# One projection of a two-layer block on Trainium2: seven half-width block products instead of eight, with the weight sums on GpSimd

## The chip, the core and the metric

The kernel runs on one core of a Trainium2 chip (trn2). The metric is the device time of one execution in microseconds (us); lower is better. Three executions of the kernel before took 1381.69, 1382.02 and 1382.20 us; their median is 1382.02 us. Engines: PE is TensorE, DVE is VectorE, ACT is ScalarE, POOL is GpSimd, SP is SyncE, which here only issues DMAs.

## What is computed

Two transformer layers over 512 tokens of width 1024, float32 in and out. The first layer has a gated linear attention and a dilated attention and then this feed-forward part, the only one that the change touches:

```python
nm = rmsnorm(h, mlp_norm_g[l])
a = jnp.square(jax.nn.relu(jnp.einsum('bsd,df->bsf', nm, w_ff1[l])))
h = h + jnp.einsum('bsf,fd->bsd', a, w_ff2[l])
```

The hidden width is 4096.

The second layer (stick-breaking attention, HGRN2, a gated feed-forward part) follows and ends the kernel.

## The kernel before, in words

**Layout.** Activations lie transposed: a row of 128 features on the partitions, 512 tokens (S) along them. `hT` holds the residual stream h as 8 such rows.

**Three products for one.** Every large product is made of rounded operands (float32r). A weight W is split in a high part `WH` (rounded) and a low part `WL` = W - WH; an activation X in `XH` and `XL` likewise. Each 128 x 128 block of weights costs three matmuls: WH·XH, WH·XL and WL·XH (lines 538, 542, 545, the inner lines of `products` in `tensor`).

**Units and pieces.** `Plan` (lines 99 to 209) cuts all weights in units of 256 output columns over 8 blocks of 128 rows. A unit is two tiles (`t`), each of which accumulates 8 blocks in one PSUM bank of 512 tokens: 2 x 8 x 3 = 48 matmuls of 128 x 512. The weights of a unit come in two pieces of 4 blocks (1024 columns, 512 KB). Plan gives each tile a time in units of three matmuls (one block); the other engines' work is ordered by such times. A generator yields the time at which its next instruction is due, and `merge` (lines 72 to 82) sorts the streams of one engine by them. These times fix only the order in each engine's queue: on the chip an instruction starts when the one before it and the semaphores that it waits for let it.

**The way of a piece.** SP loads it from HBM into one of three `RAW` buffers (line 1925). ACT rounds it into one of `HL` = 5 `WH` buffers (line 861, `splits`), once the piece five before it has been used by PE (`("product", "block", ...)`). ACT then writes the negated high part into `WL` (line 869, `negated`), and POOL issues a DMA that adds the original weight from HBM onto it (line 1881, `lows`, `accum_op=ALU.add`). This addition is done by the DMA engines, so each piece is read from HBM twice. `split_time` and `low_time` give the times of these steps, from the time at which the piece five before is used.

**The first feed-forward part.** 4096 hidden features in four groups of 1024. For group g, stage `("f1", g)` (4 units of `w_ff1`) gives 8 rows; `relu2` takes each out of PSUM on DVE (line 1572), squares it (line 1062) and rounds it (line 1064) on ACT into `AH1`, and subtracts on DVE (line 1575) for `AL1`. Stage `("f2", g)` (4 units of `w_ff2`) multiplies by these and adds each tile to `hT` on DVE (line 1559, `to_h`). Products go round three PSUM banks `GB`; four more, `FB`, serve the attention stages.

Of the kernel before, what the change touches and what calls it, by code (L numbers as in the profile page):

```python
# [29 lines left out]
DOWN = [(0, 8), (8, 16), (16, 22)]  # L30

# [53 lines left out]
class Tile:  # L85


    def __init__(self, g, u, c, i, st, kt, cols, sets, v0, v1):
        self.g, self.u, self.c, self.i, self.st = g, u, c, i, st
        self.kt, self.cols, self.sets, self.v0, self.v1 = kt, cols, sets, v0, v1  # L90

# [7 lines left out]
class Plan:  # L99
# [3 lines left out]
    def __init__(self):  # L103
# [16 lines left out]
        for g in range(4):  # L120
            add(("f1", g), "w_ff1", 4 * g, 4 * g + 4, 8, UC)
            add(("f2", g), "w_ff2", 4 * g, 4 * g + 4, 8, UC)
# [16 lines left out]
        for u, (st, name, i, kt, cols, k0) in enumerate(units):  # L139
            self.first.append(len(self.pieces))  # L140
            n = max(1, PIECE // cols)
            ends = [0, 1, 2, 4, 6, 8] if u == 0 else [*range(0, kt, n), kt]
# [7 lines left out]
        paired = {0, next(u for u, unit in enumerate(units) if unit[0] == "wo2")}  # L150
        for u, (st, name, i, kt, cols, k0) in enumerate(units):
            nat = st in NATURAL
# [29 lines left out]
    def order(self):  # L182

        for tiles in self.together:
            kt = tiles[0].kt
# [10 lines left out]
            if many:  # L196
                for t in tiles:
                    for k in (kt - 2, kt - 1):
                        for part in range(3):
                            yield t, k, part  # L200

# [29 lines left out]
def build_program(nc, A, out):  # L231
    with ExitStack() as ctx:
# [78 lines left out]
        AH1, AL1, ft1 = rows_of("AH1", 8, F32R), rows_of("AL1", 8, F32R), two("ft1", 6)  # L311
        acc2 = ft1[3]

# [42 lines left out]
        for st in plan.stage:  # L356
# [6 lines left out]
            elif st[0] == "f2":  # L363
                operands[st] = (AH1, AL1, ("f1", st[1]))
# [26 lines left out]
        def low(p):  # L391


            return ("low_first" if p < ADDED else f"low_added{p % HL}", p)
# [5 lines left out]
                    for n, p in enumerate((p for p in range(len(plan.pieces)) if p not in loaded), -EARLY)}  # L400
# [22 lines left out]
        ob = {"free": None}  # L423

# [33 lines left out]
        def low_time(p):  # L458
            return split_time(p) + (9.5 if p in loaded else 3.0 if p >= ADDED else 0.05)

# [37 lines left out]
        def tensor():  # L498
# [9 lines left out]
            def products():  # L508
                for t, k, part in plan.order():
                    XH, XL, x = operands[t.st]  # L510
# [40 lines left out]
                    elif t.c == t.sets - 1 and (k in last_k or whole):  # L551
                        mm.then_inc(*pe.sig("product", "block", t.u, k))

# [272 lines left out]
        def scalar():  # L826
# [24 lines left out]
            def splits():  # L851
                for p, (u, k, m) in enumerate(plan.pieces):
# [3 lines left out]
                    n = m * plan.units[u][4]  # L856
                    act.wait_ge((f"raw{raw_slot[p]}", p))
                    if p >= HL:
                        u0, k0, m0 = plan.pieces[p - HL]
                        act.wait_ge(("product", "block", u0, k0 + m0 - 1))  # L860
                    e.activation(WH[p % HL][:, 0:n], RAW[raw_slot[p]][:, 0:n], ACT.Copy).then_inc(*act.sig("high", p))  # L861

            def negated():
                for p, (u, k, m) in enumerate(plan.pieces):
                    if p >= ADDED:
                        yield split_time(p) + (8.0 if p in loaded else 1.5)
                        n = m * plan.units[u][4]
# [189 lines left out]
            def relu2(g):  # L1057
                def one_(t):
# [5 lines left out]
                    e.activation(AH1[:, t.i, :], f, ACT.Copy).then_inc(*act.sig(*hi(("f1", g), t.i)))  # L1064
# [182 lines left out]
        def vector():  # L1247
# [314 lines left out]
            def relu2(g):  # L1562
                def one_(t):
# [3 lines left out]
                    if t.i >= 3:  # L1567
                        dve.wait_ge(lo(("f1", g), t.i - 3))
                    elif g:
                        dve.wait_ge(lo(("f1", g - 1), t.i + 5 if t.i < 3 else 0))  # L1570
                        dve.wait_ge(lo(("f1", g - 1), 7))
                    e.scalar_tensor_tensor(f, bank_for(t), 0.0, rs, ALU.max, ALU.mult).then_inc(*dve.sig("evac_v", t.g))
                    yield due(t, 3.0)
                    dve.wait_ge(hi(("f1", g), t.i))
                    e.tensor_tensor(AL1[:, t.i, :], f, AH1[:, t.i, :].bitcast(F32), ALU.subtract).then_inc(*dve.sig(*lo(("f1", g), t.i)))
                return [one_(t) for t in plan.stage["f1", g]]

            def gain_product():
                yield plan.start(("f2", 3))
                dve.wait_ge(*x_in(0), lo(("f1", 0), 0))  # L1580
# [264 lines left out]
            for g in range(4):  # L1845
                streams += relu2(g)
                before = "mlp" if g == 0 else ("f2", g - 1)
                streams += [to_h(("f2", g), "second" if g == 3 else ("f2", g), lambda k, b=before: ("h", b, k))]
# [20 lines left out]
        def gpsimd():  # L1869
            e = pool.e  # L1870

            def lows():
                for p, (u, k, m) in enumerate(plan.pieces):
                    if p < ADDED:
# [3 lines left out]
                    n = m * cols  # L1878
                    src = A[name] if i is None else A[name][i]
# [179 lines left out]
```

## Time and profile before

| what | value |
|---|---|
| median of three executions | 1382.02 us |
| the profiled execution | 1382.6 us |
| its span, first to last instruction | 1381.3 us |
| PE busy | 1372.7 us (99%) |
| DVE, ACT, POOL busy | 629.1, 838.9, 211.5 us |
| read from HBM | 236.28 MB |
| first feed-forward part, four groups | 257.6 to 605.8 us of the span |

All rows that follow are of the one profiled execution. A matmul's duration includes the time in which it drains, and the next one starts before that; so the distance between the starts of two matmuls, not the duration, tells what one costs. "PEld" is the loading of weights into the array, which runs beside the matmul before it. In a timeline a row gives start, duration, engine, line, operation, operands, and in square brackets how long the engine was idle before and what released it.

### The profile page before, as it was taken

The numbers are of one execution on the slowest core, as the hardware profiler recorded it, in microseconds if no ns is written. First come the engines' busy times: TensorE is split into PE (matmuls) and PEld (weight loads), VectorE is DVE, ScalarE is ACT, GpSimd is POOL, SyncE is SP. The second block draws the span as 40 slices with busy tenths as digits, with TensorE's granted clock in tenths as the row PEclk, the third lists the DMA queues.
The fourth block names the chain that finished last, engine by engine and source line by source line (L and its number), as shares of the span: only waits on it lengthen the run. The fifth ranks groups of instructions, "written<-read, shape, count | busy, mean of one in ns | idle before, by whom it ended". The sixth has DMA issues, their size and how long they took to land.

```text
span 1381.3 us, 17229 instructions
## 1 busy us (share of the span) xinstructions
PE 1372.7 (99%) x6682; PEld 1112.0 (81%) x6682; DVE 629.1 (46%) x1225; ACT 838.9 (61%) x1246; POOL 211.5 (15%) x259
## 2 busy tenths in 40 slices
PE   9999999999999999999999999999999999999999
PEld 6977966788888888887777878888888888888887
DVE  6055466521211212356588789975434312331341
ACT  6575666754544545666488767775566645663661
POOL 0211100111111111111211111211111111111111
PEclk9999999999999999999999999999999999999999
DMA  7976644898888888877665675768879988889885
GB/s 251 234 169 134 147 116 94 182 195 188 196 191 196 194 194 193 190 167 153 151 133 123 135 192 123 141 150 174 199 177 212 195 193 193 190 196 194 193 169 122
DMA packets 68326, 239.53 MB, mean 173 GB/s; under 512 B 7602, under 2 KB 7915, under 8 KB 68116
## 3 DMA queue, kind: packets, MB, share of 16 engines
q0 software_dynamic: 36144, 130.32, 52.3%
q1 hardware_dynamic: 31236, 106.24, 24.2%
q10 hardware_dynamic: 864, 1.87, 0.4%
q8 instruction: 53, 0.87, 0.2%
q14 instruction: 29, 0.24, 0.1%
HBM read 236.28 MB, written 2.12 MB: 173 GB/s over the span
## 4 chain that ended last, share of the span: by engine, by line
PE 95%; DMA 2%; ACT 2%; DVE 1%; issue 0%; SPq 0%; ACTq 0%
PE bank L538 29%; PE bank L545 28%; PE bank L542 28%; PE bank L705 2%; PE bank L681 2%; PE bank L695 1%; PE bank L662 1%; DMA WL<-in_w_in 1%; PE bank L730 1%; DMA WH<-in_w_in 1%; DMA RAW<-in_w_in 1%; PE bank L713 0%; ACT WH L861 0%; PE bank L642 0%; PE bank L763 0%
## 5 line engine op out<-in xcount | busy, mean ns | idle before, releaser
L538 PE MATMUL bank<-NH,WH 128*128 128x512 f32 x1152 | 463.2, 403 | 0.3 <-ACT NH L1042 0.3
L542 PE MATMUL bank<-NL,WH 128*128 128x512 f32 x1152 | 448.2, 390 | 0.5 <-DVE NL L1272 0.5
L545 PE MATMUL bank<-NH,WL 128*128 128x512 f32 x1152 | 448.0, 390 | 0.4 <-DVE WL L1267 0.4
L861 ACT ACTIVATE WH<-RAW 128x1024 fp32r<-128x1024 f32 (+3 forms) x196 | 202.0, 1032 | 194.8 <-PE bank L545 186.6
L538 PEld LDWEIGHTS bank<-NH,WH 128*128 128x128 f32 x1152 | 216.4, 188 | 62.1 <-issue 19.3
L545 PEld LDWEIGHTS bank<-NH,WL 128*128 128x128 f32 x1152 | 216.2, 188 | 46.6 <-DVE WL L1267 0.8
L542 PEld LDWEIGHTS bank<-NL,WH 128*128 128x128 f32 x1152 | 216.7, 188 | 45.3 <-issue 2.6
L869 ACT ACTIVATE WL<-WH 128x1024 fp32r<-128x1024 f32 (+2 forms) x219 | 229.4, 1048 | 24.2 <-DMA WH<-in_w_in 19.1
L542 PE MATMUL bank<-AL,WH 128*128 128x512 f32 x432 | 168.2, 389 | 0.0
L545 PE MATMUL bank<-AH,WL 128*128 128x512 f32 x432 | 168.1, 389 | 0.0
L538 PE MATMUL bank<-AH,WH 128*128 128x512 f32 x432 | 168.1, 389 | 0.0
L1559 DVE TENSOR_TENSOR gains_hT<-gains_hT,bank 128x512 f32<-128x512 f32 x80 | 54.8, 686 | 223.4 <-PE bank L545 223.4
L1881 POOL DMA_DIRECT2D WL<-in_w_ff x64 | 55.5, 866 | 295.7 <-ACT WL L869 295.7
L1881 POOL DMA_DIRECT2D WL<-in_w_in x58 | 51.1, 891 | 297.2 <-ACT WL L869 297.1
L542 PEld LDWEIGHTS bank<-AL,WH 128*128 128x128 f32 x432 | 81.1, 188 | 17.2 <-DVE AL L1830 0.3
L538 PEld LDWEIGHTS bank<-AH,WH 128*128 128x128 f32 x432 | 81.1, 188 | 16.8
L545 PEld LDWEIGHTS bank<-AH,WL 128*128 128x128 f32 x432 | 81.1, 188 | 16.8
L1881 POOL DMA_DIRECT2D WL<-in_w_gu x44 | 38.1, 867 | 201.7 <-ACT WL L869 201.7
L538 PE MATMUL bank<-WH,NH 128*128 128x256 f32 (+2 forms) x224 | 67.9, 311 | 0.0
L545 PE MATMUL bank<-WL,NH 128*128 128x256 f32 (+2 forms) x224 | 65.0, 299 | 1.0 <-DMA WL<-in_w_in 1.0
L542 PE MATMUL bank<-WH,NL 128*128 128x256 f32 (+2 forms) x224 | 64.9, 298 | 0.0
L799 ACT ACTIVATE ft<-ft 128x512 f32<-128x512 f32 x22 | 13.9, 632 | 66.2 <-DVE ft L1813 66.2
(342 smaller groups left out, 1645.0 us busy)
## 6 DMA issues: line engine op xcount, KB each, us to landing
RAW<-in_w_ff SPq DMA_DIRECT2D x64, 512.0 KB, 5.2
WL<-in_w_ff POOLq DMA_DIRECT2D x64, 512.0 KB, 8.9
WL<-in_w_in POOLq DMA_DIRECT2D x58, 512.0 KB, 7.3
RAW<-in_w_gu SPq DMA_DIRECT2D x44, 512.0 KB, 6.6
WL<-in_w_gu POOLq DMA_DIRECT2D x44, 512.0 KB, 8.7
WH<-in_w_in POOLq DMA_DIRECT2D x32, 512.0 KB, 6.5
RAW<-in_w_in SPq DMA_DIRECT2D x28, 512.0 KB, 6.8
RAW<-in_w_down SPq DMA_DIRECT2D x20, 512.0 KB, 4.9
```

The costliest lines, as they stand in the source:

```text
L538: e.matmul(o, a[0], a[1], start=(k == 0), stop=False)
L542: e.matmul(o, b[0], b[1], start=False, stop=False)
L545: mm = e.matmul(o, c[0], c[1], start=False, stop=(k == t.kt - 1))
L662: mm = e.matmul(OB[:, t0:t0 + w], vs[:, j, h * P:(h + 1) * P], a[:, a0:a0 + w], start=(n == 0), stop=(n == len(seq) - 1), skip_group_check ...
L681: mm = e.matmul(OB[po:po + 64, i * P:(i + 1) * P], vs[:, j, h * 64:(h + 1) * 64], wbuf[p][:, j * P:(j + 1) * P], start=(j == 0), stop=(j = ...
L695: mm = e.transpose(bank[:, j * P:(j + 1) * P], z[:, j * P:(j + 1) * P], ident)
L705: e.matmul(FB[p][:, 0:n], qs[64 * p:64 * p + 64, hp, i * P:(i + 1) * P], ks[64 * p:64 * p + 64, hp, 0:n], start=True, stop=True).then_inc( ...
L799: act.e.activation(e_, x, ACT.Abs).then_inc(*act.sig("sigmoid_a", key, 0))
L861: e.activation(WH[p % HL][:, 0:n], RAW[raw_slot[p]][:, 0:n], ACT.Copy).then_inc(*act.sig("high", p))
L869: e.activation(WL[p % HL][:, 0:n], WH[p % HL][:, 0:n].bitcast(F32), ACT.Copy, scale=-1.0).then_inc(*act.sig("high_negated", p))
L1559: e.tensor_tensor(hT[:, k, :], hT[:, k, :], bank_for(t), ALU.add).then_inc(*dve.sig("evac_v", t.g))
L1881: e.dma_start(WL[p % HL][:, 0:n], src[:, k * cols:(k + m) * cols], accum_op=ALU.add).then_inc(*pool.sig(f"low_added{p % HL}", p, by=16))
```

## The change

In the first three of the four groups of `("f2", g)`, a unit of 256 output columns is computed by a scheme of the Strassen-Winograd kind. The unit's weight is seen as 2 x 2 quarters (A11, A12, A21, A22: two halves of output columns by two halves of the hidden features, the features of even and odd rows), and the activations as 2 x 2 quarters: even and odd rows by the two halves of 256 tokens. Seven products of quarters (each 4 blocks x 3 matmuls of 128 x 256) take the place of eight, so a unit is 84 matmuls of 128 x 256. Each product is accumulated in a bank of `FB` (3 per unit, one of them alternating), and DVE adds the banks to `hT` in seven steps (`seven_out`), some banks between two products that accumulate in them. PE waits for these steps (`h_part`).

The weight side needs five sums or differences of 128 x 512 per unit (S1, S3, A12 + A11, S4, S2), done on POOL (`quarter_sums`). The activation side needs four sums of 128 x 256 per pair of rows, done on DVE. The unit's weights now take four pieces in the ring of five (three of 1024 columns and one of 512), of which only one still goes the old way (negated on ACT, added by a DMA of POOL); the low parts of the other three are subtractions on DVE (`quarter_rests`). SP loads the quarters into buffers of their own.

The core of the diff:

```diff
+SEVEN = [(0, S, 0, 0, "even"), (0, 0, UC, 2, "even_sum"), (1, 0, 5 * UC, 1, "odd"), (2, S, 2 * UC, 0, "odd_sum"),
+         (2, 0, 6 * UC, 2, "odd"), (1, S, 4 * UC, 1, "odd_sum"), (3, 0, 3 * UC, 0, "odd_sum")]
+SEVEN_GROUPS = 3
+OPENS = (0, 1, 2, 5)
+CLOSES = (4, 2, 5, 6)
+SEVENTH = 84 * 0.12 / 0.681 / 7
...
+                for n, last in enumerate((2, 6, 5, 7)):
+                    self.used[self.first[u] + n] = v + last * SEVENTH
...
+    def freed(self, p):
+        u, k, m = self.pieces[p]
+        return ("seven", u, (1, 5, 4, 6)[k]) if u in self.sevens else ("product", "block", u, k + m - 1)
...
+            def seven(t, n):
+                piece, w0, x0, bank, part = SEVEN[n]
+                s, g, p = plan.sevens.index(t.u), t.st[1], plan.first[t.u] + piece
+                o = FB[seven_bank(s, bank)][:, 0:UC]
...
+                if n in OPENS and s > (n == 0):
+                    pe.wait_ge({0: ("h_part", plan.sevens[s - 2], 6), 1: ("h_part", plan.sevens[s - 1], 4),
+                                2: ("h_part", plan.sevens[s - 1], 5), 5: ("h_part", t.u, 2)}[n])
+                if n in (3, 4, 5, 6):
+                    pe.wait_ge(("h_part", t.u, {3: 0, 4: 1, 5: 2, 6: 3}[n]))
+                pe.wait_ge(high(p), low(p))
+                for j in range(4):
+                    pe.wait_ge(("pair_high", g, j, part), ("pair_low", g, j, part))
...
+                    for i, (a, b) in enumerate(((wh, xh), (wh, xl), (wl, xh))):
+                        mm = e.matmul(o, a, b, start=(n in OPENS and j == 0 and i == 0),
+                                      stop=(n in CLOSES and j == 3 and i == 2), skip_group_check=True)
+                mm.then_inc(*pe.sig("seven", t.u, n))
```

ACT, per unit: four roundings in place of two, one negation in place of two. Per pair of rows of `("f1", g)`: two squares as before, and roundings of 256 (even), 256 (even_sum), 512 (odd) and 768 columns (odd_sum) in place of two of 512.

```diff
+                        act.wait_ge(plan.freed(p - HL))
+                        act.wait_ge(*[[("quarter_sum", u, "S1"), (f"quarters_1{plan.sevens.index(u) % 2}", u)],
+                                      [(f"quarters_2{plan.sevens.index(u) % 2}", u)],
+                                      [("quarter_sum", u, "S2"), ("quarter_sum", u, "S4")], [("quarter_sum", u, "S3")]][k])
+                        part = (q[:, 2 * S:4 * S], q[:, 0:2 * S], quarters_s, q[:, 4 * S:5 * S])[k]
+                        e.activation(WH[p % HL][:, 0:(S if k == 3 else 2 * S)], part, ACT.Copy).then_inc(*act.sig("high", p))
```

DVE: the sums and rests of a pair of rows, the rests of the weights, and the steps to `hT`:

```diff
+                    if t.i % 2 == 0:
+                        difference(0, T1, f[:, UC:], f[:, 0:UC], ("relu_square", g, t.i), *back)
+                        rest("even", f[:, 0:UC])
+                        yield due(t, 4.5)
+                        rest("even_sum", T1)
+                    else:
+                        difference(1, T2, f[:, UC:], T1, ("relu_square", g, t.i), ("pair_sum", g, j, 0))
+                        difference(2, T3, f[:, UC:], x1[:, UC:])
+                        difference(3, T4, f[:, 0:UC], T2, ("pair_sum", g, j, 1))
+                        rest("odd", f)
+                        yield due(t, 4.5)
+                        rest("odd_sum", sums1[:, UC:4 * UC])
...
+            def quarter_rests(g):
...
+                    yield split_time(p) + 1.6
+                    rest(0, q[:, 2 * S:4 * S])
+                    yield split_time(p + 2) + 1.6
+                    rest(2, quarters_s)
+                    yield rests_time(u)
+                    rest(3, q[:, 4 * S:5 * S])
...
+            def seven_out(g):
...
+                    for n, (row, ts, bank, back) in enumerate(steps):
+                        yield t.v0 + SEVENTH * (n + 1) + 0.8
+                        dve.wait_ge(("seven", u, n), ("h", *before, row), *(("h_part", u, i) for i in back))
+                        e.tensor_tensor(hT[:, row, ts], hT[:, row, ts], bank, ALU.add).then_inc(*dve.sig("h_part", u, n))
```

POOL and SP:

```diff
+            def quarter_sums(u):
...
+                yield split_time(p) - 5.0
+                add("S1", S1, A22, A21, ALU.add, (f"quarters_2{s}", u), (f"quarters_1{s}", u))
+                yield split_time(p) - 3.0
+                add("S3", A21, A11, A21, ALU.subtract, ("quarter_sum", u, "S1"))
+                yield split_time(p) + 0.5
+                n = plan.sevens.index(u)
+                back = [("low_sum", plan.first[plan.sevens[n - 1]] + 2)] if n else []
+                add("A12 + A11", S4, A12, A11, ALU.add, *back)
+                yield split_time(p) + 2.5
+                add("S4", S4, S4, S1, ALU.subtract, ("quarter_sum", u, "A12 + A11"))
+                yield split_time(p) + 4.5
+                add("S2", S2, S1, A11, ALU.subtract)
...
+                            if s >= 2:
+                                sp.wait_ge(("low_sum", plan.first[back] + 3), ("high", plan.first[back] + 1))
...
+                            e.dma_start(q[:, 0:2 * S], src[:, 0:2 * S]).then_inc(*sp.sig(f"quarters_2{s % 2}", u, by=16))
+                            e.dma_start(q[:, 3 * S:5 * S], src[:, 2 * S:4 * S]).then_inc(*sp.sig(f"quarters_1{s % 2}", u, by=16))
```

There are two sets of quarter buffers, so the quarters of a unit are loaded (`back` is the unit two before) once that unit's last rest is done. The host lays `w_ff2` out by quarters for the first three groups. The fourth group, and everything else, runs as before.

## Rows read from the trace of the kernel before

**Rows 1.** The page: span, busy time of each engine, granted clock of PE.

```profile
span 1381.3 us, 17229 instructions
PE 1372.7 (99%) x6682; PEld 1112.0 (81%) x6682; DVE 629.1 (46%) x1225; ACT 838.9 (61%) x1246; POOL 211.5 (15%) x259
...
PEclk9999999999999999999999999999999999999999
```

**Rows 2.** Windows of the changed stages, f2 of groups 0, 1, 2.

```profile
core 0: us, PE busy (x) PEld busy (x) DVE busy (x) ACT busy (x) POOL busy (x), PEclk, DMA share, GB/s
301.13:344.65 43.52, 43.52 (x193) 36.04 (x192) 6.20 (x9) 18.13 (x18) 6.93 (x9) 1.00 0.89 193
388.17:431.69 43.52, 43.52 (x193) 36.04 (x192) 6.20 (x9) 18.12 (x18) 6.96 (x9) 1.00 0.87 193
475.21:518.73 43.52, 43.52 (x193) 36.04 (x192) 6.20 (x9) 18.13 (x18) 6.93 (x9) 1.00 0.89 194
```

**Rows 3.** What PE waited for, from 257 to 606 us: us, times, longest.

```profile
PE bank L542 <- DVE NL L1272: 0.5, 2, 0.3
PE bank L538 <- ACT NH L1042: 0.3, 1, 0.3
```

**Rows 4.** Timeline of PE where f2 of group 0 ends.

```profile
344.20 0.39 PE L542 MATMUL bank<-AL,WH 128*128 128x512 f32 x1
344.43 0.39 PE L545 MATMUL bank<-AH,WL 128*128 128x512 f32 x1
344.65 0.39 PE L538 MATMUL bank<-NH,WH 128*128 128x512 f32 x1
```

**Rows 5.** Timeline of PE and PEld in an earlier stage with 256 columns.

```profile
47.83 0.28 PE L538 MATMUL bank<-WH,NH 128*128 128x256 f32 x1
47.95 0.28 PE L542 MATMUL bank<-WH,NL 128*128 128x256 f32 x1
48.07 0.28 PE L545 MATMUL bank<-WL,NH 128*128 128x256 f32 x1
...
47.83 0.19 PEld L542 LDWEIGHTS bank<-WH,NL 128*128 128x128 f32 x1
47.95 0.19 PEld L545 LDWEIGHTS bank<-WL,NH 128*128 128x128 f32 x1
```

**Rows 6.** Line 1267 on DVE: ns min/median/max, for 256, 512 and 1024 columns.

```profile
L1267 DVE TENSOR_TENSOR WL<-RAW,WH x9: 419/693/1225, 6.3 to 23.6; 128x512 fp32r<-128x512 f32 x3, 128x256 fp32r<-128x256 f32 x2, 128x1024 fp32r<-128x1024 f32 x2, 128x816 fp32r<-128x816 f32 x2
```

**Rows 7.** Groups of DVE and ACT instructions by line, 301 to 606 us.

```profile
L1559 DVE TENSOR_TENSOR gains_hT<-gains_hT,bank 128x512 f32<-128x512 f32 x32 | 22.0, 687 | 110.6 <-PE bank L545 110.6
L869 ACT ACTIVATE WL<-WH 128x1024 fp32r<-128x1024 f32 x56 | 59.4, 1061 | 1.8
L861 ACT ACTIVATE WH<-RAW 128x1024 fp32r<-128x1024 f32 x56 | 59.3, 1060 | 92.6 <-PE bank L545 92.6
L1064 ACT ACTIVATE AH<-ft 128x512 fp32r<-128x512 f32 x25 | 15.8, 632 | 0.8
```

**Rows 8.** Timeline around the first f1 tile of group 1: how long hand-overs take.

```profile
344.91 1.06 ACT L861 ACTIVATE WH<-RAW 128x1024 fp32r<-128x1024 f32 x1 [0.57 <-PE bank L545]
346.00 1.06 ACT L869 ACTIVATE WL<-WH 128x1024 fp32r<-128x1024 f32 x1
347.36 0.87 POOL L1881 DMA_DIRECT2D WL<-in_w_ff  x1 [1.85 <-ACT WL L869]
350.29 0.69 DVE L1572 SCALAR_TENSOR_TENSOR ft<-bank,rs 128x512 f32<-128x512 f32 x1 [4.75 <-PE bank L545]
351.02 0.63 ACT L1062 ACTIVATE ft<-ft 128x512 f32<-128x512 f32 x1 [3.95 <-DVE ft L1572]
351.68 0.63 ACT L1064 ACTIVATE AH<-ft 128x512 fp32r<-128x512 f32 x1
352.35 0.69 DVE L1575 TENSOR_TENSOR AL<-ft,AH 128x512 fp32r<-128x512 f32 x1 [1.36 <-ACT AH L1064]
```

**Rows 9.** All POOL instructions that read SBUF, and DVE around them.

```profile
46.75 1.26 POOL L1901 CAST marks<-cu_f 128x896 uint8<-128x896 f32 x1
47.97 1.89 POOL L1903 CAST resets<-cu_f 128x1664 uint8<-128x1664 f32 x1
...
32.56 0.69 DVE L1357 TENSOR_TENSOR kG<-bank,rs 128x512 f32<-128x512 f32 x1 [0.85 <-PE bank L545]
51.34 0.68 DVE L1346 COPY glT<-bank 16x512 f32<-16x512 f32 x1 [18.09 <-PE bank L598]
```

**Rows 10.** Line 1881 from 301 to 606 us: issue and landing.

```profile
L1881 POOL DMA_DIRECT2D WL<-in_w_ff x53: 866/866/884, 301.1 to 584.9; - x53
...
DMA to landing us min/median/max: 6.1/9.0/10.4
```

**Rows 11.** Line 1881 from 640 to 706 us, where few DMAs run together.

```profile
L1881 POOL DMA_DIRECT2D WL<-in_w_in x7: 862/881/889, 668.0 to 704.2; - x7
L1881 POOL DMA_DIRECT2D WL<-in_w_vs x3: 866/866/866, 643.6 to 658.8; - x3
...
DMA to landing us min/median/max: 5.5/6.4/8.3
```

**Rows 12.** The page: DMA queues with packets, MB, share of 16 engines.

```profile
q0 software_dynamic: 36144, 130.32, 52.3%
q1 hardware_dynamic: 31236, 106.24, 24.2%
```

**Rows 13.** Line 1575 on DVE over the whole span: ns min/median/max.

```profile
L1575 DVE TENSOR_TENSOR AL<-ft,AH x32: 691/693/695, 270.7 to 565.9; 128x512 fp32r<-128x512 f32 x32
```

More of the change, by code:

```diff
@@ L90, in __init__ @@
         self.kt, self.cols, self.sets, self.v0, self.v1 = kt, cols, sets, v0, v1
+        self.seven = st[0] == "f2" and st[1] < SEVEN_GROUPS
 NATURAL = {"vG", "vD", "vS", "vH"}
@@ L150, in __init__ @@
         paired = {0, next(u for u, unit in enumerate(units) if unit[0] == "wo2")}
+        self.sevens = [u for u, unit in enumerate(units) if unit[1] == "w_ff2"]
         for u, (st, name, i, kt, cols, k0) in enumerate(units):
+            if u in self.sevens:
+                mine = self.stage.setdefault(st, [])
+                for c, last in enumerate((5, 7)):
+                    t = Tile(len(self.tiles), u, c, len(mine), st, kt, cols, 2, v, v + last * SEVENTH)
+                    self.tiles.append(t)
+                    mine.append(t)
+                self.together.append(mine[-2:])
+                for n, last in enumerate((2, 6, 5, 7)):
+                    self.used[self.first[u] + n] = v + last * SEVENTH
+                v += 7 * SEVENTH
+                continue
             nat = st in NATURAL
@@ L184, in order @@
         for tiles in self.together:
+            if tiles[0].seven:
+                for n in range(7):
+                    yield tiles[0], n, None
+                continue
             kt = tiles[0].kt
@@ L363, in build_program @@
             elif st[0] == "f2":
[L364 removed]
+                operands[st] = (AH1_last, AL1_last, ("f1", st[1]))
             elif st[0] == "dn":
@@ L399, in build_program @@
         raw_slot = {p: p if p < EARLY else n % RAWS
-                    for n, p in enumerate((p for p in range(len(plan.pieces)) if p not in loaded), -EARLY)}
+                    for n, p in enumerate((p for p in range(len(plan.pieces)) if p not in loaded and plan.step(p) is None), -EARLY)}
         def high(p):
@@ new lines, in one_, with rest, difference @@
+                    j = t.i // 2
+                    T1, T2, T3, T4 = (sums1[:, i * UC:(i + 1) * UC] for i in range(4))
+                    def rest(part, x):
+                        lo_, hi_ = PART[part]
+                        dve.wait_ge(("pair_high", g, j, part))
+                        e.tensor_tensor(AL1[j][:, lo_:hi_], x, AH1[j][:, lo_:hi_].bitcast(F32),
+                                        ALU.subtract).then_inc(*dve.sig("pair_low", g, j, part))
+                    def difference(n, to, a, b, *waits):
+                        dve.wait_ge(*waits)
+                        e.tensor_tensor(to, a, b, ALU.subtract).then_inc(*dve.sig("pair_sum", g, j, n))
```

139 lines of the change are left out of this document (118 added, 21 removed).

## The prediction, made before the changed kernel was run

> **What bounds the kernel now.** I read the page first: PE is busy 1372.7 of 1381.3 us, at the full granted clock (2.4 GHz) throughout [rows 1]. Then the windows of the stages that change: in each 43.52 us long f2 stage PE is busy for all of it, DVE 6.2, ACT 18.1, POOL 6.9 us, and the DMA engines 0.87 to 0.89 [rows 2]. Then the waits: PE waits 0.8 us in all between 257 and 606 us [rows 3]. So PE's stream of matmuls is the time here, and whatever shortens it is gained, as long as nothing else becomes late. The reader should see two things: this stage has almost no waits to win, and it stays so because weights are prepared far ahead: a piece is used 27 us after its buffer comes free (five pieces of 5.44 us). Between this profiled execution (1382.6 us, span 1381.3) and the median (1382.02) lie 0.6 us; I add my sum to the median.
>
> **What PE gains.** Matmuls of 512 columns start 0.227 us apart [rows 4], so a unit of 48 takes 10.88 us (x 4 = 43.52, the stage). With 256 columns, a new weight block each time, they start 0.120 us apart, and the 0.19 us weight loads overlap [rows 5]. A unit of 84 is 10.08 us. Gain 0.80 us per unit, 12 units: **9.6 us**, 3.2 per group.
>
> **What the other engines get.** A sum of 512 columns on DVE is 0.69 us, one of 256 is 0.42, of 1024 1.23 [rows 6]; ACT takes 1.06 for 1024 and 0.63 for 512 [rows 7], so by the slope 0.42 and 0.84 for 256 and 768. Per f2 unit: DVE three rests (1.23 + 1.23 + 0.69) and seven adds to hT (6 x 0.42 + 0.69) = 6.4 us instead of 1.4; ACT 3 x 1.06 + 0.63 + 1.06 = 4.9 instead of 4.2; both of 10.08, so neither is full. Per pair of f1 rows (10.88 us): DVE 5.6 instead of 2.8, ACT 3.6 instead of 2.5 beside 4.2 for weights; hidden unless a row is awaited. DMA: of four transfers of 512 KB one adding one goes. From the page an adding MB costs 0.523 x 1381 / 130.3 = 5.5 us of the 16 engines, a plain one 3.1 [rows 12]; a unit falls from 9.1 to 6.2 us of DMA time. SP issues two plain loads per unit as before.
>
> POOL gets five sums of 128 x 512 per unit, an operation that the trace lacks. The nearest rows are POOL's casts: 896 columns 1.26 us, 1664 columns 1.89 [rows 9], that is 0.53 + 0.00082 per column. Bounds: 0.95 us (512 columns) and 1.37 us (two inputs read one after the other, 0.53 + 1024 x 0.00082). I take 1.37, since there are two inputs. Then POOL works 5 x 1.37 + 0.87 = 7.7 of 10.08 us. [...]
>
> **Three places where work gets late.** A unit now fills four of five buffers, so pieces are prepared one unit ahead rather than 2.5.
>
> (a) *The hand-over between units.* The third weight piece is free after product 5 of the unit before. From there to product 3, which waits for DVE's first add: hand-over 0.2 and rounding 1.06 [rows 8], then in DVE's queue rest 2 (1.23), rest 3 (0.69), the last add of the unit before (0.69), rest 0 of the unit after (1.23), the first add (0.42), 0.1 to PE: 5.7 us. Products 3 to 5 take 4.3. The loop closes in 10.0 of 10.08 us: it hides, with no slack at all. Rest 0 waits besides for POOL's S1, for which the quarters are loaded only after an earlier rest 3.
>
> (b) *The start of f2.* The last row of f1 passes through DVE and ACT: 0.2 + 0.69 + squaring 0.67 [rows 8], but on ACT the rounding for the next unit stands before the squaring, and on DVE its rest (together 2.5 us after the end of f1); then three differences (1.3) and the odd rest (0.69) give 4.5 us. Product 2 wants that row after 2 x 1.44 + 1.08 = 3.96 us. Late by **0.6 us** per group; before, the slack was 4.8 against 3.0.
>
> (c) *The one piece that still goes through DMA.* Free after product 1, needed at product 2 of the next unit: exactly 10.08 us. Chain: 0.2 + 1.06 + 1.1 + 0.3 [rows 8] + landing. Landing took 9.0 us (median) when DMAs were crowded [rows 10], 6.4 where few ran [rows 11]: 11.7 or 9.1 us. With the load down by a third and the quarters' loads just before it I take 7 to 8: late by 0 to 0.6 in most units, about 0.7 per group. And at the start of the next f1 three pieces come free nearly together (after products 4 to 6), each needing rounding, negation and such a DMA, where the queue is crowded: the second f1 unit starts about **1.5 us** late. Sum of (b) and (c) 2.8 us per group: it eats nearly all of the 3.2.
>
> **The unknown that decides: DVE beside POOL.** DVE's rests and differences read two tensors from SBUF, and POOL's sums read SBUF too. No row shows the two together: at the only POOL instructions that read SBUF (46.8 to 49.9 us) DVE is idle until 51.34 [rows 9]. POOL's DMA issues leave DVE alone (691 to 695 ns over all 32 [rows 13]), but these issue, they don't stream. Bounds for what a DVE rest loses beside a sum: 0 and the rest of one whole sum, 1.37. I take the upper kind, each waiting for the other, because the sums stand at the very moments of the rests, and the issues are the more distant case. The Trainium skill, SBUF — State Buffer, Who interferes with whom, says just this: a DVE instruction with two SBUF inputs contends with a GpSimd one that reads SBUF, and the second waits for the first to finish. No run here shows it yet; by it the time below follows, without it 1381.
>
> Priced by rows: in (a) rest 2 and rest 0 each wait for the remainder of a sum, 0.7 on average with rest 3 at times, less what the late quarters spread: 1.9 us in each of two hand-overs per group (the last unit has no next one). In (b) POOL does the second unit's five sums ahead, among the small differences of the last f1 rows, which alternate with them: five waits of up to 1.37, 6.9 us, less some 4 us that DVE idles per pair (10.88 - 5.6 - 1.2): 3 us more. Per group: 2.8 + 3.8 + 3.0 - 3.2 = 6.4, but a unit that is late at one place is less late at the next; I take 5.7, three groups **17 us**: 1399.
>
> **The rivals.** (1) *It doesn't contend, and the waits of (b) and (c) cancel the gain*: 1382.0 - 9.6 + 3 x 2.8 = 1380.8, from 1376.5 to 1386 with landings of 6.4 and 9 us. For it: the loads fit on every engine. (2) *The gain arrives*: landings of 6.4 us, no late f1, only (b): 1382.0 - 9.6 + 1.8 = 1374. For it: DMA load falls by a third; against: the chain of (c) has only 1 us even then. Decides where an adding DMA lands within 7 us. (3) *POOL becomes the bound*: if a sum and the rests exclude each other for long, POOL's 7.7 us and DVE's 3.2 us of two-input work add up to 10.9 per unit, and the DMA issue behind S2 is late, which delays product 2 for every unit: 12 to 12.5 us a unit, 1382 + 12 x 1.4 + 3 x 5 = 1414. For it: POOL issues that DMA only after the next unit's sums. (4) That the change doesn't do what it says can only be so in PE's pitch; [rows 5] speak against it.
>
> **Numbers.** About 0.2% (2.8 us) can be told from no change. Forecast case 0.48 (its own range 1388 to 1410), rival 3 0.10, rival 1 0.27, rival 2 0.15. Of rival 1 a third lies faster than 1379.3, some 0.13 within the bound, the rest slower. Faster 0.25, same 0.13, slower 0.62. The range leaves out half of rival 2 and the far end of rival 3: 1375 to 1415.
>
> **What would show it.** In the profile after: matmuls of 256 columns at 0.120 us pitch, or PE's part is wrong. Line 1267-like rests on DVE of 1024 columns: 1.23 us each when they don't contend, up to 2.6 when they do; POOL sums 1.37, or longer beside DVE. PE's waits in f2: on an add to hT before product 3 (a), on the odd row at the start (b), on the adding DMA before product 2 and in the first two f1 units (c). If the rests keep to 1.23 us, the forecast falls to rival 1 or 2, and the landing of the adding DMA in f2 tells which. If f2 stages are under 41.5 us and f1 stages 43.5, I was wrong on all three places.

## The result, and the profile after

The changed kernel takes 1404.07 us (median of 4 executions, 1402.04 to 1405.68), the kernel before 1382.11. The ratio is 1.0159, 95% interval 1.0141 to 1.0176: 1.6% slower. The forecast was 1399 us, with a chance of 0.62 on slower. The profiled execution has a span of 1404.4 us.

The windows of the stages that [rows 2] show for before, now f2 and f1 in turn (columns: start:end, length, busy time and count of PE, PEld, DVE, ACT, POOL, granted clock, DMA share, GB/s), and below them two short windows out of the first, at half and at full granted clock:

```profile
300.05:351.35 51.30, 43.48 (x337) 43.10 (x336) 32.70 (x52) 24.12 (x29) 24.04 (x19) 0.90 0.55 136
351.35:397.23 45.88, 43.84 (x194) 35.97 (x193) 26.00 (x32) 25.65 (x33) 21.18 (x17) 1.00 0.72 173
397.23:445.61 48.38, 42.55 (x337) 41.99 (x336) 28.22 (x49) 23.28 (x28) 19.72 (x16) 0.96 0.58 142
445.61:490.71 45.10, 44.15 (x194) 35.89 (x193) 26.01 (x32) 25.66 (x33) 21.32 (x17) 1.00 0.72 175
490.71:539.84 49.13, 44.43 (x337) 43.54 (x336) 28.75 (x49) 23.29 (x28) 19.70 (x16) 0.93 0.57 141
539.84:584.58 44.74, 43.84 (x194) 35.96 (x193) 10.46 (x16) 28.21 (x33) 7.81 (x10) 1.00 0.94 222
...
308.30:314.30 6.00, 6.00 (x28) 6.00 (x29) 5.89 (x11) 4.68 (x7) 0.00 (x0) 0.50 0.57 175
314.35:320.00 5.65, 5.65 (x50) 5.65 (x49) 1.85 (x5) 1.92 (x3) 3.50 (x3) 1.00 0.59 85
```

An f2 stage should take 40.3 us instead of 43.5; it takes 51.3, 48.4 and 49.1. The f1 stages behind them take 45.9, 45.1 and 44.7 instead of 43.5. That is 18.3 us more in f2 and 5.2 in f1. No other part of the program lengthened.

PE's waits in these stages (engine and line waited for: us in total, times, longest us), where [rows 3] had 0.8 us:

```profile
PE bank L638 <- DVE AL L1704: 11.0, 3, 7.0
PE bank L638 <- DMA WL<-in_w_ff: 4.6, 3, 2.0
PE bank L609 <- DMA WL<-in_w_ff: 3.9, 4, 2.0
PE bank L638 <- ACT AH L1171: 2.6, 1, 2.6
```

Line 638 is the new matmul, 609 the old one (here in f1), 1704 the rest of an activation part, 1171 its rounding. The first and fourth row are one thing, the start of f2: PE waits for the parts of the last two f1 rows, in all three groups at the fourth block of product 0, and in group 1 once more at the fourth block of product 2. The timeline of PE shows the pitch of the new matmuls before the longest wait, and after it:

```profile
300.89 0.28 PE L638 MATMUL bank<-AL,WH 128*128 128x256 f32 x1
301.01 0.28 PE L638 MATMUL bank<-AH,WL 128*128 128x256 f32 x1
...
308.25 0.55 PE L638 MATMUL bank<-AH,WH 128*128 128x256 f32 x1 [6.97 <-DVE AL L1704]
...
308.82 0.42 PE L638 MATMUL bank<-AH,WL 128*128 128x256 f32 x1
309.03 0.41 PE L638 MATMUL bank<-AH,WH 128*128 128x256 f32 x1
```

The pitch is 0.12 us as in [rows 5]; so PE's part of the change is as promised. After 7 idle us it is 0.21 us: the granted clock has fallen to 0.50 (1.2 GHz), and 28 matmuls take the 6.0 us in which 50 would fit.

What DVE and POOL did meanwhile (start, duration; line 1737 is the rest of a weight piece, 1709 a difference of activations, 1691 takes an f1 tile out of PSUM, 2087 is a weight sum):

```profile
296.53 2.61 DVE L1737 TENSOR_TENSOR WL<-quarters_s,WH 128x1024 fp32r<-128x1024 f32 x1 [1.97 <-ACT WH L956]
299.06 1.50 DVE L1709 TENSOR_TENSOR sums<-ft,sums 128x256 f32<-128x256 f32 x1
300.49 1.50 DVE L1709 TENSOR_TENSOR sums<-ft,ft 128x256 f32<-128x256 f32 x1
301.91 1.48 DVE L1709 TENSOR_TENSOR sums<-ft,sums 128x256 f32<-128x256 f32 x1
303.31 1.75 DVE L1704 TENSOR_TENSOR AL<-ft,AH 128x512 fp32r<-128x512 f32 x1
304.99 0.94 DVE L1704 TENSOR_TENSOR AL<-sums,AH 128x768 fp32r<-128x768 f32 x1
```

```profile
298.12 2.16 POOL L2087 TENSOR_TENSOR quarters<-quarters 128x512 f32<-128x512 f32 x1
300.25 1.46 POOL L2087 TENSOR_TENSOR quarters_s<-quarters 128x512 f32<-128x512 f32 x1
301.79 1.33 POOL L2087 TENSOR_TENSOR quarters_s<-quarters_s,quarters 128x512 f32<-128x512 f32 x1
303.07 1.44 POOL L2087 TENSOR_TENSOR quarters_s<-quarters 128x512 f32<-128x512 f32 x1
```

The two engines step in turn: each of the three differences ends 0.3 us behind the end of a sum of POOL. A difference of 256 columns takes 0.42 us by [rows 6], here 1.50; a rest of 1024 takes 2.61 in place of 1.23; as soon as POOL's sums end (304.5), the 768-column rest takes its plain 0.94. Groups 1 and 2 show the same sequence with the same durations, but earlier: in group 0 the long rest starts 3.5 us before f2 (296.53 against 300.05), in group 1, below, 8.0 us before it (f2 starts at 397.23), and in group 2 also 8.0.

```profile
389.24 2.61 DVE L1737 TENSOR_TENSOR WL<-quarters_s,WH 128x1024 fp32r<-128x1024 f32 x1 [1.96 <-ACT WH L956]
```

The adds to hT, which read one tensor from SBUF and one from PSUM, aren't touched, though some run beside sums (ns min/median/max, of lines 1760 and 1709 over the whole span):

```profile
L1760 DVE TENSOR_TENSOR gains_hT<-gains_hT,bank x72: 407/421/422, 312.6 to 538.6; 128x256 f32<-128x256 f32 x72
...
L1709 DVE TENSOR_TENSOR sums<-ft,sums x24: 411/423/2304, 272.5 to 497.9; 128x256 f32<-128x256 f32 x24
L1709 DVE TENSOR_TENSOR sums<-ft x12: 424/426/427, 269.0 to 493.5; 128x256 f32<-128x256 f32 x12
L1709 DVE TENSOR_TENSOR sums<-ft,ft x12: 417/1500/1512, 274.7 to 497.6; 128x256 f32<-128x256 f32 x12
```

### The profile page after: what moved, and what is told of

Same layout as the page of the kernel before. It is cut to its first block, busy times and chain, and to the rows that moved or that the text cites. A ratio compares the mean times of both kernels' runs of the same rounds, so it can differ in the third digit from the quotient of the medians.

```text
span 1404.4 us, 18455 instructions
## 1 busy us (share of the span) xinstructions
PE 1374.3 (98%) x7114; PEld 1132.2 (81%) x7114; DVE 746.2 (53%) x1393; ACT 854.4 (61%) x1282; POOL 293.2 (21%) x307
## 4 chain that ended last, share of the span: by engine, by line
PE 79%; DVE 7%; DMA 5%; ACT 5%; issue 2%; POOL 1%; SPq 0%; ACTq 0%; DVEq 0%
PE bank L602 23%; PE bank L609 22%; PE bank L606 22%; PE bank L638 4%; DMA WL<-in_w_ff 4%; DVE sums L1709 2%; PE bank L796 1%; PE bank L753 1%; PE bank L772 1%; DMA WH<-in_w_in 1%; POOL quarters_s L2087 1%; PE bank L786 1%; ACT WH L956 1%; DVE AL L1704 1%; PE bank L821 1%
## 5 line engine op out<-in xcount | busy, mean ns | idle before, releaser
L961 ACT ACTIVATE WH<-RAW 128x1024 fp32r<-128x1024 f32 (+3 forms) x172 | 176.2, 1027 | 122.0 <-PE bank L609 100.3
L638 PE MATMUL bank<-AH,WH 128*128 128x256 f32 x336 | 99.5, 296 | 18.3 <-DVE AL L1704 11.0
L1677 DVE TENSOR_TENSOR gains_hT<-gains_hT,bank 128x512 f32<-128x512 f32 x56 | 38.3, 686 | 119.7 <-PE bank L609 119.7
L638 PE MATMUL bank<-AL,WH 128*128 128x256 f32 x336 | 98.3, 293 | 0.0
L638 PE MATMUL bank<-AH,WL 128*128 128x256 f32 x336 | 98.2, 292 | 0.0
L638 PEld LDWEIGHTS bank<-AH,WH 128*128 128x128 f32 x336 | 67.8, 202 | 20.3 <-ACT AH L1171 12.6
L2076 POOL DMA_DIRECT2D WL<-in_w_ff x44 | 38.3, 870 | 179.6 <-ACT WL L969 179.3
L606 PE MATMUL bank<-AL,WH 128*128 128x512 f32 x176 | 68.6, 390 | 0.0
L609 PE MATMUL bank<-AH,WL 128*128 128x512 f32 x176 | 68.5, 389 | 0.0
L602 PE MATMUL bank<-AH,WH 128*128 128x512 f32 x176 | 68.5, 389 | 0.0
```

The costliest lines, as they stand in the source:

```text
L602: e.matmul(o, a[0], a[1], start=(k == 0), stop=False)
L606: e.matmul(o, b[0], b[1], start=False, stop=False)
L609: mm = e.matmul(o, c[0], c[1], start=False, stop=(k == t.kt - 1))
L638: mm = e.matmul(o, a, b, start=(n in OPENS and j == 0 and i == 0), stop=(n in CLOSES and j == 3 and i == 2), skip_group_check=True)
L1677: e.tensor_tensor(hT[:, k, :], hT[:, k, :], bank_for(t), ALU.add).then_inc(*dve.sig("evac_v", t.g))
L2076: e.dma_start(WL[p % HL][:, 0:n], src[:, k * cols:(k + m) * cols], accum_op=ALU.add).then_inc(*pool.sig(f"low_added{p % HL}", p, by=16))
```

## The experiments

Two theories stood after this: **exclusion** (a DVE instruction with two SBUF inputs and a POOL instruction that reads SBUF don't run together) and **lateness** (POOL is slow, or DVE has too much to do, or the order is bad, and the long durations only go with it).

**e1: POOL busy, but not reading.**

```diff
-                    e.tensor_tensor(to, a, b, op).then_inc(*pool.sig("quarter_sum", u, key))
+                    for i in range(2):
+                        e.memset(to, 0.0).then_inc(*pool.sig("written", u, key, i))
+                        pool.wait_ge(("written", u, key, i))
+                    e.memset(to, 0.0).then_inc(*pool.sig("quarter_sum", u, key))
```

> Each of POOL's five sums per unit is replaced by three memsets of its destination in a row (0.53 us each in the trace of before, so some 1.6 to 1.8 us for the three, no faster than the 1.45 to 1.95 us that a sum took after). POOL then reads no SBUF there; the weight sums are left out of what is computed. Theory (DVE's two-input instructions and POOL's SBUF reads exclude each other): DVE's differences go back from 0.90 and 1.05 to 0.42 us, the 1024-column rests from 1.62 and 1.75 to 1.23, the stalls of 7.0, 2.6 and 2.7 us at the start of f2 shrink to under 1 each, the half clock goes with them; the waits on the adding DMA (8.5 us in all) stay or shrink a little: 1386 to 1391 us. Rival (POOL is simply too slow and its results come late, whatever it reads): stalls stay, 1400 to 1406 us.

1384.69 us, ratio to before 1.0014 (1.0004 to 1.0024), a little under the 1386 to 1391 expected. With POOL as occupied as before (three memsets take about 1.7 us), DVE's durations are plain (line 1709 on DVE, ns min/median/max):

```profile
L1709 DVE TENSOR_TENSOR sums<-ft,sums x24: 414/418/426, 273.5 to 479.4; 128x256 f32<-128x256 f32 x24
...
L1709 DVE TENSOR_TENSOR sums<-ft,ft x12: 415/417/419, 273.8 to 479.0; 128x256 f32<-128x256 f32 x12
```

PE's waits at the start of f2 are 0.5 us in all three groups together:

```profile
PE bank L638 <- DVE AL L1704: 0.5, 3, 0.2
```

The clock stays at 1.00. Exclusion holds, lateness of POOL falls: 19.4 of the 22 us go with the reads alone. What the adding DMA costs stays in the main (6.3 us of waits, 8.5 in the change).

**e8: POOL reads one input instead of two.**

```diff
-                    e.tensor_tensor(to, a, b, op).then_inc(*pool.sig("quarter_sum", u, key))
+                    e.tensor_copy(to, a).then_inc(*pool.sig("quarter_sum", u, key))
```

> The changed kernel with each POOL sum replaced by a POOL copy of its first input to the same place: one SBUF input instead of two; the sums are left out of what is computed. Theory (any POOL instruction that reads SBUF excludes a DVE instruction with two SBUF inputs, for its whole length): DVE's 256-column differences still cost more than 0.42 us, by about the length of a POOL copy (0.7 to 0.95 us by the casts), and the adds to hT, with one SBUF input, stay at 0.42 us. A form between: 1390 to 1397 us. Rival (it takes two inputs on both engines): DVE at 0.42 us throughout, 1385.

1387.03 us, a single execution, so the durations count here more than the time. Lines 1709 and 1760 on DVE, and the copies of one kind on POOL:

```profile
L1709 DVE TENSOR_TENSOR sums<-ft,ft x12: 417/826/830, 273.9 to 479.9; 128x256 f32<-128x256 f32 x12
...
L1760 DVE TENSOR_TENSOR gains_hT<-gains_hT,bank x72: 414/421/422, 305.6 to 520.4; 128x256 f32<-128x256 f32 x72
...
L2087 POOL COPY quarters<-quarters x24: 616/698/1518, 272.7 to 495.4; 128x512 f32<-128x512 f32 x24
```

A DVE difference lost 0.41 us beside a copy of 0.6 to 0.7 us, and 1.08 beside a sum of 1.3 to 1.5: so one input of POOL is enough, and the shorter POOL instruction costs DVE less. The time came below the 1390 to 1397 that I had written; copies are shorter than I had them (0.61 against 0.7 to 0.95).

**e2: the sums on DVE**, `quarter_sums` moved to DVE's streams with all its due times, `pool.` replaced by `dve.`.

> The five sums per unit run on DVE with the same due times, POOL only issues DMAs. A DVE sum costs 0.69 us, five 3.45 per unit, less than the 1.1 us that each POOL sum took from DVE in the changed kernel (5 x 1.1 = 5.5). Theory (exclusion): rests and differences at 0.42 and 1.23 us, stalls at the start of f2 under 2 us each; but S1 and S3 now stand in DVE's queue waiting for the quarters' load, before adds to hT, so some of PE's waits go to hT in the middle units: 1386 to 1398. Rival (DVE's queue is the bound, not the port): DVE gets 3.4 us more per unit, the stalls grow, over 1404.

1385.71 us, 1.0028 (1.0017 to 1.0039), 18.4 us faster than the change, just under the 1386 to 1398 that exclusion gave. All sums are computed here, each in 0.68 us. DVE got 3.4 us more work per unit, and PE still waited for it less. PE's waits are now spread: 2.2 us on adds to hT, 3.4 on the adding DMA, 1.2 on a rounding.

**e4: the clock alone.** PE gets matmuls into an unused bank ahead of the wait at the start of f2.

```diff
+                    if s % 4 == 0 and n == 0 and j == 3:
+                        for _ in range((48, 16, 16)[g]):
+                            e.matmul(OB[:, 0:UC], WH[p % HL][:, w], AH1[0][:, 0:UC], start=True, stop=True)
```

> PE gets matmuls of 256 columns into an unused bank right before the wait at the start of f2: 48 in group 0 (5.8 us of a 7.1 us wait), 16 in groups 1 and 2 (1.9 us of 2.7). They fit in the waits, so they cost nothing. Theory (the half clock of 10.2, 3.4 and 3.4 us after those waits costs time of its own, since 256 columns start every 0.23 us there): these stretches go and 3 to 6 us come back: 1398 to 1401. Rival (the time at half clock is covered by the waits that follow, on DVE and the DMA): 1404 within 1 us.

1400.50 us, 1.0138 (1.0123 to 1.0153) to before: 3.6 us came back, within the 3 to 6 expected. The f2 stages are at full clock throughout:

```profile
300.19:351.27 51.08, 46.83 (x385) 46.27 (x384) 32.66 (x52) 24.12 (x29) 24.09 (x19) 1.00 0.56 139
395.47:442.77 47.30, 42.98 (x354) 42.43 (x352) 29.59 (x49) 24.05 (x29) 20.68 (x16) 1.00 0.59 147
487.13:534.04 46.91, 43.20 (x353) 42.47 (x352) 29.02 (x49) 23.32 (x29) 19.97 (x16) 1.00 0.60 146
```

That is 0.2, 1.1 and 2.2 us less than in the change, 3.5 in all. Group 0, which had the longest stretch at half clock (10.2 us), got almost nothing back: PE waits for the next activation part (1.5 us, at 313.05) and for the adding DMA (1.5 us) instead. So the half clock cost about 3.6 us, and the rest of it was covered by waits that came anyway.

**e3: other time, same engine.** The second unit's sums were to be done before the last f1 rows, into a second buffer.

```diff
-                yield split_time(p) - 5.0
+                yield split_time(p) - ahead[0] - 5.0
                 add("S1", S1, A22, A21, ALU.add, (f"quarters_2{s}", u), (f"quarters_1{s}", u))
...
-                S4, S2 = quarters_s[:, 0:S], quarters_s[:, S:2 * S]
+                S4, S2 = quarters_s[s][:, 0:S], quarters_s[s][:, S:2 * S]
```

> Only the time and place of the second unit's five sums change: they are done some 14 to 18 us earlier, in the middle of f1, into a second buffer for S4 and S2 (the squares' buffers, free then), so that POOL does no sum beside the differences of the last f1 rows. All is computed. Theory (the stall at the start of f2 is the alternation of POOL's sums with the last rows' small DVE instructions): of the 12.3 us waited at the start of f2 in three groups, under 3 are left, and the half clock with it, 5 us or so: 1404 - 9 - 4 = 1389 to 1393. Rival (DVE's own work for the last rows is too long, with rest 0 and rest 2 in its queue): 1399 or more.

1403.01 us, 1.0162 (1.0129 to 1.0195): nothing gained, the rival's number. It doesn't prove the rival, since the edit didn't do what I wanted: POOL takes its queue in order, and the sums stood behind an adding DMA that was issued at 282.8 us, so they ended at 296.4 (304.5 in the change) instead of 14 to 18 us earlier. They now collided with the rows before; the three differences that took 1.5 us each take 0.42 here, but start at 301.3, no earlier than in the change. The stall at the start of f2 was 5.3 us instead of 7.1 in group 0, and 6.1 us of waits on hT were new. A miss; it shows that a due time on POOL is worth only what its queue ahead of it allows.

**e12: the loads beside the adding DMA.** The change with one wait more on SP, before the first of the next group's f1 weights.

```diff
+                    if st[0] == "f1" and 1 <= st[1] <= SEVEN_GROUPS and i % 4 == 0 and k == 0:
+                        sp.wait_ge(low(plan.first[plan.sevens[4 * st[1] - 2]] + 1))
```

> The changed kernel with one edit: SP loads the next group's f1 weights only when the adding DMA of the third unit has landed. Theory (term c in f2 is that crowd of loads): the waits of 0.9, 1.8 and 2.0 us before product 2 of the fourth unit, for the adding DMA issued beside those loads, go or halve, and so does the half clock behind two of them; the first f1 pieces may come later. 1404.1 - 2 to - 5 us: 1399 to 1402. Rival (the DMA is late because POOL issues it late, behind S2): 1403 to 1405.

(Where it says fourth unit, it is the third: at 332.9 us two products of it have run.) 1397.22 us, 1.0106 (1.0086 to 1.0126), 6.9 us faster than the change, more than the 2 to 5 expected. All waits on the adding DMA in f2 (4.6 us) are gone though POOL issues it behind the same sums, and the start of f2 is as bad as ever (14.5 us, the longest 7.0).

**e5: no adding DMA at the start of f1**, on top of e2: the first four pieces get their low part from DVE.

```diff
+            def direct_rests():
+                for p in sorted(direct):
+                    yield split_time(p) + 1.6
+                    dve.wait_ge(("high", p))
+                    e.tensor_tensor(WL[p % HL], RAW[raw_slot[p]], WH[p % HL].bitcast(F32), ALU.subtract).then_inc(*dve.sig("low_sum", p))
```

> Beside the sums on DVE (1385.7 us), the first four weight pieces of the next group's f1 get their low part from a DVE subtraction of 1.23 us instead of negation and adding DMA (in the three groups behind a changed f2 stage). These are the pieces that come free together at the end of f2. Theory (c): PE's wait of 0.9, 0.6 and 0.9 us in the first f1 unit and what follows it, 1.1 us per f1 stage in all, goes: 1385.7 - 3.3 = 1382 to 1383. Rival (the buffers come free too late whatever the way, the DMA only shows it): 1385 or more.

1381.92 us, 0.9997 (0.9987 to 1.0006): level with the kernel before, and 3.8 us faster than e2, as the theory had it. The three f1 stages took 43.5 us each.

**e6 and e7: order, first try.** On e2 (e6) and on e5 (e7): ACT rounds the DMA's piece first, SP as in e12, and DVE's rest 0 and the sums later (three of them are shown by one line).

```diff
+                turned = [p + 1 if plan.step(p) == 0 else p - 1 if plan.step(p) == 1 else p for p in range(len(plan.pieces))]
...
-                    yield split_time(p) + 1.6
+                    yield split_time(p + 1) + 3.6
                     rest(0, q[:, 2 * S:4 * S])
...
-                yield split_time(p) + 0.5
+                yield split_time(p) + 8.0
```

> Sums on DVE, and only the order of the queues changes: ACT rounds the piece that goes through the DMA before the first piece, DVE does rest 0 and the sums of the next unit after the first adds to hT, SP loads the next group's f1 weights only when the adding DMA of the third unit has landed. Theory: what is left of PE's waits in f2 comes from order alone (hT 2.2 us in all, DMA and rounding 2.7, at the start about 1): at least half goes, 1385.7 - 3 = 1382 to 1384. Rival (DVE with 9.9 of 10.08 us is the bound in the middle units, so a wait that goes at one place returns at another): 1385 to 1388.

> The two before together. If they act on different waits, their gains add up: 1379 to 1381, for the first time below the kernel before (1382). If DVE is the bound, 1383 or more.

1393.83 us (1.0078, 1.0061 to 1.0096) and 1387.73 us (1.0041, 1.0029 to 1.0054): both slower than what they were built on (1385.71 and 1381.92), and outside what I had expected, 1382 to 1384 and 1379 to 1381. The waits on the DMA in f2 were gone, but my due times had put rest 0 and three sums (3.3 us) in one block between the third and the fourth add to hT, which PE waits for: 11.1 us of waits, nine times, in each of the two.

**e9: spread.** As e7, with one long DVE instruction after each add and S1 and S3 back at their times of e2. **e10** is e9 without the wait on SP.

```diff
-                    yield split_time(p) + 1.6
+                    yield max(split_time(p) + 7.1, split_time(p + 1) + 1.9)
                     rest(0, q[:, 2 * S:4 * S])
...
-                yield split_time(p) + 0.5
+                yield split_time(p) + 5.0
...
-                yield split_time(p) + 2.5
+                yield split_time(p) + 9.2
                 add("S4", S4, S4, S1, ALU.subtract, ("quarter_sum", u, "A12 + A11"))
-                yield split_time(p) + 4.5
+                yield split_time(p) + 11.4
```

> Sums on DVE, f1's first four pieces without the adding DMA, ACT's order and SP's late f1 loads as in e7 (which left no wait on a DMA), but DVE's long instructions are spread one by one between the adds to hT: A12 + A11 after the second, rest 0 after the third, S4 after the fourth, S2 after the fifth. In e6 and e7 three of them stood together before the fourth add (11.1 us of waits). Theory (exclusion gone, what is left is order): waits on hT under 3 us in all, none on the DMA: 1376 to 1379, below the kernel before. Rival (DVE with 9.9 of 10.08 us can't be ordered so that no add is late): 1381 or more.

> As e9, but SP loads f1's weights as early as in the changed kernel, beside the adding DMA of the third unit. Theory (that DMA is late because of three 512 KB loads beside it: it landed in 7.6 us against 5.9 in its neighbours): 0.5 to 1.5 us of wait before product 2 of the third unit in each group come back, e9 + 2 to + 4 us. Rival (ACT's order alone removed it): the same as e9 within 1 us.

e9: **1372.05 us, 0.9925 (0.9910 to 0.9939)**, faster than the kernel before by 0.75%, and below the 1376 to 1379 that I had expected. Its windows of f2, f1 and f2:

```profile
300.98:341.42 40.44, 40.44 (x337) 40.38 (x336) 32.76 (x58) 19.14 (x22) 2.60 (x3) 1.00 0.61 156
341.42:384.97 43.55, 43.55 (x195) 36.04 (x193) 27.33 (x47) 25.96 (x35) 4.32 (x5) 1.00 0.61 146
384.97:425.41 40.44, 40.44 (x338) 40.36 (x336) 32.75 (x58) 19.14 (x22) 2.59 (x3) 1.00 0.61 157
```

PE is busy for the whole of both, f2 takes the 336 x 0.12 us that its matmuls need, and of waits only 0.7 us are left, of the kind of [rows 3]. So the whole gain of 9.6 us is there, with DVE at 32.8 of 40.4 us.

e10: 1385.41 us, 1.0024 (1.0014 to 1.0035), 13 us slower for the lack of one wait on SP (expected 2 to 4). The adding DMA at 315.73 us, right behind three loads of 512 KB and the quarters', landed after 10.3 us; the one in its place in e9, at 316.57, behind the quarters' loads alone, after 5.8 (the last line of the view of the adding DMA, for e10 and then for e9):

```profile
DMA to landing us min/median/max: 10.3/10.3/10.3
```

```profile
DMA to landing us min/median/max: 5.8/5.8/5.8
```

PE waited 2.8 to 3.0 us for it in each group, and half clock followed twice. In the profiled execution the three f2 stages took 43.4, 45.0 and 44.9 us; the waits and the two stretches at half clock account for the 11.9 us over e9's.

**e11: e9 with the sums back on POOL**, same places.

> The fastest version so far (1372.1 us), with one thing undone: the five sums run on POOL again, at the same places in the order. Theory (exclusion is what costs, order only decides how much of it shows): the stall at the start of f2 comes back in part, DVE's differences at 0.9 to 1.1 us and rests at up to 1.7; between 1378 and 1392 us, at least 6 slower than with the sums on DVE, though POOL's sums take 3.4 us per unit off DVE. Rival (with this order the engine that sums doesn't matter): 1372 to 1375.

1430.20 us, 1.0353 (1.0331 to 1.0374): 58 us for one engine instead of the other, nearly three times the largest I had expected (20 us). POOL's and DVE's timelines where product 3 of the second unit waits for an add to hT:

```profile
314.85 1.59 POOL L2098 TENSOR_TENSOR quarters_s<-quarters_s,quarters 128x512 f32<-128x512 f32 x1
316.10 1.57 POOL L2098 TENSOR_TENSOR quarters<-quarters 128x512 f32<-128x512 f32 x1
317.34 1.54 POOL L2098 TENSOR_TENSOR quarters_s<-quarters 128x512 f32<-128x512 f32 x1
318.56 1.54 POOL L2098 TENSOR_TENSOR quarters<-quarters 128x512 f32<-128x512 f32 x1
```

```profile
314.92 6.27 DVE L1748 TENSOR_TENSOR WL<-quarters,WH 128x1024 fp32r<-128x1024 f32 x1 [1.36 <-ACT WH L961]
321.11 1.26 DVE L1771 TENSOR_TENSOR gains_hT<-gains_hT,bank 128x256 f32<-128x256 f32 x3
```

One rest of 1.23 us took 6.27: it began 0.07 us after the first of four sums, and all four went ahead of it. None of the last three waits for the one right ahead of it, and each starts 0.3 us before that one's end. Behind the rest stood three adds to hT, which need nothing from POOL. PE lost 31.2 us on adds to hT, in nine waits, and 9.4 us on activation parts; seven stretches at half clock followed. The theory had the direction, not the size.

## Why the prediction was right, and where it was not

**Held.** PE's gain: 0.12 us pitch, 9.6 us, shown by e9's stages of 40.44. Direction and mechanism: exclusion of DVE's two-input instructions and POOL's sums, which the trace of before couldn't show. The Trainium skill, SBUF — State Buffer, Who interferes with whom, has this rule, and e1, e8 and the untouched adds agree with it in which inputs count and in that it is the reading that does it. That the later instruction waits only for the one that runs, e11 does not bear out (see the last section). A POOL sum took 1.27 to 1.29 us at least, between my 0.95 and 1.37. ([rows 9] leave out a third cast on POOL, 256 columns in 0.73 us; it lies on the line that the other two give.)

**Term (a), the hand-over, was wrong.** I priced it at 1.9 us in each of two hand-overs per group, 11.4 us in all, and PE waited 0.3 us, once. I had rest 2 and rest 0 collide with sums there. But A12 + A11 waits for rest 2 to end, so POOL comes after DVE and not beside it; rest 2 keeps to 1.23 us in all but one of these hand-overs, and rest 3 to 0.69. The order of semaphores kept them apart, which I could have read in the diff. Only rest 0 collides, and loses 0.5 us (DVE, and POOL beside it, in a hand-over of group 0):

```profile
322.17 1.72 DVE L1737 TENSOR_TENSOR WL<-quarters,WH 128x1024 fp32r<-128x1024 f32 x1
```

```profile
321.13 1.68 POOL L2087 TENSOR_TENSOR quarters_s<-quarters 128x512 f32<-128x512 f32 x1 [2.25 <-DVE WL L1737]
322.89 2.16 POOL L2087 TENSOR_TENSOR quarters_s<-quarters_s,quarters 128x512 f32<-128x512 f32 x1
```

The first add behind it ends at 324.24, and product 3 starts at 324.30: the loop took the 0.5 us with nothing to spare. e11, where rest 0 meets four sums, shows what (a) costs then.

**Term (b), the start of f2, was too small.** Forecast 3.6 us per group (0.6 + 3.0), 10.8 in all; measured, as the distance of two starts less a pitch, 7.1, 4.4 and 2.7, together 14.2. The mechanism is the one forecast, POOL's sums for the second unit among DVE's differences, but the place is another: I had only the last row late, at product 2, while DVE was still at the rows before, and PE stopped in product 0 in every group. The 2.61 us rest and the differences at 1.5 are the same in all groups; group 0 stalls longest because DVE comes to them 4.5 us later. The profile shows two things behind that. DVE takes group 0's first f1 tile out of PSUM only when the scale of the normalisation is there, 32.5 us before f2 starts, and in group 1, which has the scale, 37.9 before. And in group 0 S1 and S3 of the first unit run beside the differences of an earlier pair (from 272.5 us: 2.30 and 1.51 us in place of 0.42), while in groups 1 and 2 POOL waits for the quarters' load there and the same differences take 0.42. How much each adds to the 7.1 us no run tested.

**Term (c), the adding DMA.** Per group 0.7 in f2 and 1.5 in f1, 6.6 in all; measured 1.0, 1.9 and 2.1 in f2 (5.1) and 5.2 more in the f1 stages. The size in f1 was about right (4.5 forecast), but the waits stand in the first f1 unit and not before the second; in f2 I had the quarters' loads as the crowd, while it is the next group's f1 weights, which SP requests three at once (e12, e10).

**Not foreseen: the clock.** 3.6 us (e4). The forecast had nothing for it.

Sum: forecast -9.6 + 11.4 + 10.8 + 6.6 = 19.2, taken as 17; measured -9.6 + 0.3 + 14.2 + 10.3 and for the clock 3.6 to 8 (the f2 stages less their matmuls and waits leave 8.3) make 19 to 23, against 22. That 1399 came within 5 us of 1404 is partly luck: (a) too much by 11, (b), (c) and the clock too little by about as much.

**Open.** e10's median lies 1.4 us further above e9's than its profiled execution does; that part isn't explained. What makes the clock fall after one wait and not after another of the same length isn't shown either.

## What to carry to other kernels

Don't give POOL elementwise work that reads SBUF beside a DVE that has instructions with two SBUF inputs on the critical path: moving the sums onto the busier-looking DVE was worth 18 us, and it is not POOL's share (21% of the span) but whom it holds that counts. When a product gets shorter, the buffers ahead of it must cover the longest preparation (here a DMA that adds), and what else the DMA engines are given in that moment is part of the order. With all queues in order, one long instruction after each that PE waits for, not three in a block, turned 1387.7 into 1372.1 us.

## What was not expected of the hardware

- A DVE instruction that waits for POOL's read doesn't get its turn after one POOL instruction. It waited 5.0 us for four sums, none of which waited for the one right ahead of it (e11); in the changed kernel a difference lost 1.08 us, less than one sum. Why the four went first isn't shown: sums that follow without a wait are the likely condition, but no run varied that alone.
- The adding DMA beside three loads: 10.3 us against 5.8 (e10, e9).
- The granted clock fell to 0.50 after waits of 1.8, 2.0 and 2.5 us within a dense stream of matmuls of 256 columns (after: 3.4 us each). The length of the wait alone doesn't tell: in the same profile it stayed at 1.00 after one of 2.6 us (at 401.04), in e1 after the one of 2.7 us below, and of three waits of 1.8 us on the same add two were followed by half clock in e6 and none in e7. After the waits of up to 1.2 and 1.4 us in e2 and e5 it stayed at 1.00.

```profile
414.24 0.35 PE L638 MATMUL bank<-AH,WH 128*128 128x256 f32 x1 [2.69 <-DMA WL<-in_w_ff]
```
